# Two transformer blocks on one core: another order of the weight ring, and products placed ahead of two barriers

## The reference

```
first block:
  ada = silu(c) @ w_ada + b_ada -> shift, scale, gate     (three times 1024)
  p = (rms(x) * (1 + scale) + shift) @ w_in               (1024 x 3600)
  o_a = rms(gated_linear_attention(...)) * gla_norm_w * silu(a_gate)      4 heads
  o_b = rms(gated_linear_attention(...)) * hgrn_norm_w * silu(b_gate)     4 heads
  o_c = stick_breaking_attention(q, k, v) * silu(c_gate)                  4 heads
  x = rms(x + gate * (concat(o_a, o_b, o_c) @ w_out)) * final_norm_w
second block:
  h = rms(x) * norm_mix; projections by w_in_2 (1024 x 2824)
  att = rms(sliding_window_attention(att_q, att_k, att_v)) * norm_att_out
  hm  = rms(sigmoid(ml_gate) * mlstm(ml_q, ml_k, ml_v, ml_if)) * norm_ml_out
  x += concat(att, hm) @ w_out_2
  x += cross_attention(rms(x) * norm_cross, rms(mem) * norm_mem)
  x += mixture_of_experts(rms(x) * norm_ffn)              32 experts, top 2
  out = rms(x) * norm_final
```

## Time and profile before

| what | us |
|---|---|
| median of 3 runs (2258.09 to 2258.85) | 2258.72 |
| the profiled execution | 2257.62 |
| its span on the core | 2255.8 |
| PE busy, share of the span | 2114.3, 94% |
| DVE busy | 864.4 |
| ACT busy | 557.1 |
| POOL busy | 250.0 |
| mean granted TensorE clock, share of full | 0.975 |

### The profile page before, as it was taken

One profiled execution on the slowest core, in us unless ns is written; L12 is line 12 of the kernel. 1 busy time (PEld: TensorE's weight loads), 2 busy tenths in 40 slices (PEclk: granted clock), 3 DMA queues, 4 the chain that ended last, 5 costly groups with the idle time before them and its releaser, 6 DMA issues.

```text
span 2255.8 us, 38154 instructions
## 1 busy us (share of the span) xinstructions
PE 2114.3 (94%) x15824; PEld 1179.1 (52%) x15824; DVE 864.4 (38%) x1492; ACT 557.1 (25%) x1009; POOL 250.0 (11%) x252
## 2 busy tenths in 40 slices
PE   6999999999899989999989999999899999999996
PEld 4445555655334434654446454566566666665553
DVE  2225540545565730685446562134511111111115
ACT  3022322323563210342123211043011111111112
POOL 0013420433330000000000000000000000000002
PEclk9999999999899989999999999999799999999998
DMA  8212111101404042101110302100499999999996
GB/s 302 100 47 70 61 47 37 52 29 64 128 1 149 28 162 70 38 5 70 38 38 1 140 1 75 40 19 38 168 380 410 408 407 408 410 410 410 407 361 231
DMA packets 110277, 353.08 MB, mean 157 GB/s; under 512 B 18904, under 2 KB 59504, under 8 KB 97264
## 3 DMA queue, kind: packets, MB, share of 16 engines
q1 hardware_dynamic: 65168, 274.98, 31.6%
q0 software_dynamic: 14688, 54.53, 6.5%
q10 hardware_dynamic: 30336, 22.42, 3.1%
HBM read 310.75 MB, written 41.16 MB: 156 GB/s over the span
## 4 chain that ended last, share of the span: by engine, by line
PE 38%; DMA 11%; DVE 4%; issue 1%; ACT 1%; ACTq 0%; DVEq 0%; PEldq 0%
PE bank L598 17%; DMA y_of_slot<-HT 10%; PE bank L1173 8%; PE bank L1189 4%; PE bank L1007 2%; PE bank L654 1%; DVE work L1754 1%; DVE O L1760 1%; PE bank L1179 1%; PE bank L1164 1%; PE bank L1101 0%; PE bank L594 0%; ACTq L1682 0%; PE bank L981 0%; DVE work L1757 0%
## 5 line engine op out<-in xcount | busy, mean ns | idle before, releaser
L598 PE MATMUL bank<-slots,HT 128*128 128x512 f32 (+3 forms) x1088 | 372.0, 500 | 0.1
L598 PE MATMUL bank<-HT,slots 128*128 128x512 f32 x736 | 321.6, 599 | 3.8 <-PEq L588 1.3
L598 PEld LDWEIGHTS bank<-slots,HT 128*128 128x128 f32 x1088 | 190.1, 196 | 164.2 <-issue 160.8
L598 PEld LDWEIGHTS bank<-HT,slots 128*128 128x128 f32 x736 | 141.2, 192 | 181.9 <-issue 177.2
L1283 ACT ACTIVATE work<-bank 128x512 f32<-128x512 f32 (+5 forms) x205 | 108.6, 535 | 450.2 <-PE bank L598 271.9
L1283 ACT ACTIVATE work<-work 128x1024 f32<-128x1024 f32 (+7 forms) x199 | 158.6, 808 | 218.3 <-DVEq L143 158.2
L1283 ACT ACTIVATE HT<-bank 64x256 f32<-64x256 f32 (+2 forms) x218 | 92.8, 432 | 461.1 <-PE bank L1173 208.4
L1173 PE MATMUL bank<-slots,HT 128*32 128x256 f32 x3264 | 179.5, 379 | 2.8 <-DVE HT L2404 1.2
L2484 POOL TENSOR_TENSOR work<-work 128x1024 f32<-128x1024 f32 (+4 forms) x84 | 137.0, 1632 | 381.8 <-DVEq L143 322.0
L1173 PE MATMUL bank<-work,HT 128*32 128x256 f32 x3072 | 168.9, 379 | 0.6 <-DMA work<-in_w_e_up_dram 0.4
L1173 PEld LDWEIGHTS bank<-slots,HT 128*32 128x32 f32 x3264 | 107.6, 110 | 73.2 <-issue 6.8
(11 more groups left out here) (263 smaller groups left out, 2352.6 us busy)
## 6 DMA issues: line engine op xcount, KB each, us to landing
slots<-in_w_e_gate_dram SPq DMA_DIRECT2D x17, 2048.0 KB, 18.1
slots<-in_w_e_up_dram SPq DMA_DIRECT2D x17, 2048.0 KB, 22.8
slots<-in_w_e_down_dram SPq DMA_DIRECT2D x17, 2048.0 KB, 23.7
work<-in_w_e_gate_dram SPq DMA_DIRECT2D x16, 2048.0 KB, 18.2
work<-in_w_e_up_dram SPq DMA_DIRECT2D x16, 2048.0 KB, 22.9
work<-in_w_e_down_dram SPq DMA_DIRECT2D x16, 2048.0 KB, 23.8
slots<-in_w_in_dram SPq DMA_DIRECT2D x9, 2048.0 KB, 8.5
y_of_slot<-HT ACTq DMA_DIRECT2D x132, 96.0 KB, 24.5
```

The costliest lines, as they stand in the source:

```text
L598: ins = pe.matmul(bank, lhsT, rhs, start=(n == 0), stop=(n == len(pairs) - 1))
```

## The change

1. **Order of the weight ring.** c_qk goes ahead of ada4, ada5 goes behind a_gate, a_gate keeps its slot by two empty names (`a_gate_still`, `a_gate_last`), and all later chunks move on by one slot. PE makes the row product of ada5 after the barrier that follows linear attention a; ACT's copy of it, and the load of the gate row, move too.
2. **Values early.** V of the stick attention lies in the work area instead of HT and is loaded in one DMA right after the chunk stick_qk, ahead of out0.
3. **First mix.** ACT's Ln and Exp for the first two tiles' norms move ahead of the barrier. PE makes tile 0's out products before it turns tile 1, and hears from DVE that the stick gates are in.
4. **Queries ahead of two barriers.** The ringA fills (half 0) of att_q and of cross_q stand ahead of the last turned tile; the barrier is passed with these four banks full (`held=4`), and the ringV fills follow behind it.
5. **mLSTM.** Five of the eight first ml_gate products stand ahead of `emptied()`.
6. **Norm rows.** POOL issues both rows and the loads of x1 behind each other and waits afterwards.

```diff
@@ -293,16 +293,17 @@
         add_chunk("a_v", (w_in, 512, 1024))
-        for n in range(4, 6):
-            add_chunk(f"ada{n}", (w_ada, 512 * n, 512 * n + 512))
         add_chunk("c_qk", (w_in, 2576, 3088))
+        add_chunk("ada4", (w_ada, 512 * 4, 512 * 5))
         add_chunk("c_gate", (w_in, 3344, 3600))
         add_chunk("a_gate", (w_in, 1040, 1552))
+        add_chunk("ada5", (w_ada, 512 * 5, 512 * 6))
         add_chunk("b_qf", (w_in, 1552, 2064))
+
+        add_chunk("a_gate_still")
         add_chunk("b_v", (w_in, 2064, 2320))
-
-        add_chunk("a_gate_still")
         add_chunk("cv_bgate", (w_in, 3088, 3344), (w_in, 2320, 2576))
+        add_chunk("a_gate_last")
         ahead_dram = scratch("products_ahead", [P, 28 * HALF])
@@ -389,11 +390,13 @@
             qk = slots[:, n * NK * HALF:(n + 1) * NK * HALF]
-            Q, K, V = cut(qk[:, 0:2 * T], 2), cut(qk[:, 2 * T:4 * T], 2), HT[:, 4:6, :]
+            Q, K = cut(qk[:, 0:2 * T], 2), cut(qk[:, 2 * T:4 * T], 2)
...
             W = [[ar(HALF) for _ in range(2)] for _ in range(2)]
-            R = [[ar(HALF) for _ in range(2)] for _ in range(2)]
+            R = [[ar(HALF) for _ in range(2)]]
+            V = cut(ar(NT * 512), NT)[:, :, 256:512]
+            R.append([ar(HALF) for _ in range(2)])
             return Q, K, V, L, W, R
@@ -457,7 +460,7 @@
                   for n in range(2)]
-        GATE_CALLS = ((8, 12), (2, 4, 4), (2, 3, 3), (2, 3, 3), (0, 2, 0))
+        GATE_CALLS = ((3, 12), (2, 4, 4), (2, 3, 3), (2, 3, 3), (0, 2, 0))
         GATES_LATE = 6
@@ -582,8 +585,10 @@
-            def next_phase():
-                emptied()
+            def next_phase(held=0):
+
+                pe.wait_ge(ringA.free, ringA.filled - held)
+                pe.wait_ge(ringV.free, ringV.filled)
                 phases[0] += 1
@@ -736,7 +741,7 @@
                             if chunk == "a_gate":
-                                used("a_gate_still")
+                                used("a_gate_last")
                             ahead_over[name].append((pair, place))
@@ -820,12 +825,12 @@
-            for n in range(2):
-                row_product(f"ada{4 + n}", ringA)
+            row_product("ada4", ringA)
             emptied()
...
             next_phase()
+            row_product("ada5", ringA)
             product_fm("b_qf", 512, fm_fills(4))
@@ -851,13 +856,13 @@
                     if b == 2:
-                        pe.wait_ge(values_in, 32)
+                        pe.wait_ge(values_in, 16)
                     if at == 0 and x >= 2:
...
                     for hh in range(2):
-                        ins = pe.matmul(STICK_OUT[x % 2][64 * hh:64 * hh + 64, t0:HALF],
-                                        V[:, pair, j * P + 64 * hh:j * P + 64 * hh + 64],
+                        h = 2 * pair + hh
+                        ins = pe.matmul(STICK_OUT[x % 2][64 * hh:64 * hh + 64, t0:HALF], V[:, j, h * 64:h * 64 + 64],
                                         W[b % 2][hh][:, t0:HALF], start=(at == 0), stop=True, skip_group_check=True)
@@ -882,8 +887,9 @@
             turned = [ringA.filled]
+            hear("dve")
             for i in range(NT + 1):
-                if i + 1 < NT:
+                if 1 <= i and i + 1 < NT:
                     hear("dve")
@@ -893,13 +899,19 @@
                         used(name)
+                if i == 0:
+                    hear("dve")
+                    turn_tile(1, O[:, 1, :], ringA, SB0 // P)
+                    turned.append(ringA.filled)
+                if i == NT:
+                    product_fm("att_q", 512, [fill for fill in fm_fills(4) if fill[2] is ringA])
                 if i:
...
                     turn_tile(i - 1, NORMED[(i - 1) % 2], ringV)
-            next_phase()
-
-
-            product_fm("att_q", 512, fm_fills(4))
+            next_phase(held=4)
+
+
+            product_fm("att_q", 512, [fill for fill in fm_fills(4) if fill[2] is ringV])
             product_fm("att_kv", P, fm_fills(1))
@@ -973,7 +985,7 @@
             ringV.close(ins)
-            emptied()
+            pe.wait_ge(ringA.free, ringA.filled)
@@ -1010,6 +1022,8 @@
             ringA.use(banks[0:2])
+            gates_ahead(5)
+            emptied()
             maxima_of(0)
@@ -1062,24 +1076,26 @@
                         product_tm(name, 512, [(i, ringV)])
+                if i == NT:
+                    pe.wait_ge(ringA.free, ringA.filled)
+                    pe.wait_ge(ringD.free, ringD.filled)
+                    ringA.use(banks[0:4])
+                    product_fm("cross_q", 512, [fill for fill in fm_fills(4) if fill[2] is ringA])
                 if i:
...
                     turn_tile(i - 1, NORMED2[(i - 1) % 2], ringV)
-            emptied()
-            pe.wait_ge(ringD.free, ringD.filled)
-            ringA.use(banks[0:4])
-            next_phase()
+            next_phase(held=4)
...
             CQ, M2, MT, CK, CV, S, PT, OT = cross_area()
-            product_fm("cross_q", 512, [fill for fill in fm_fills(4) if fill[0] < 3])
+            product_fm("cross_q", 512, [fill for fill in fm_fills(4) if fill[2] is ringV and fill[0] < 3])
             hear("dve")
...
                 ringV.close(ins)
-            product_fm("cross_q", 512, [fill for fill in fm_fills(4) if fill[0] == 3])
+            product_fm("cross_q", 512, [fill for fill in fm_fills(4) if fill[2] is ringV and fill[0] == 3])
             emptied()
@@ -1427,14 +1443,15 @@
                     empty(lambda b: func(V[:, i, :], b, ACT.Copy))
-            for n in range(2):
+            def gate_of_block(n):
+
                 empty(lambda b: func(gate_row[:, n * P:(n + 1) * P], b[:, 0:P], ACT.Copy))
                 act.dma_start(gate_dram[n], gate_row[0:P:32, n * P:(n + 1) * P]).then_inc(gate_stored, 16)
+
+            gate_of_block(0)
             linear("a")
-            act.wait_ge(gate_stored, 32)
-            act.dma_start(gate_row, gate_dram.rearrange("a q n -> (a q n)").rearrange("(b n) -> b n", b=1)
-                          .partition_broadcast(P)).then_inc(gate_in, 16)
             next_phase()
+            gate_of_block(1)
@@ -1455,6 +1472,9 @@
                     empty(lambda b: func(V[:, i, 0:256], b[:, 0:256], ACT.Copy))
+            act.wait_ge(gate_stored, 32)
+            act.dma_start(gate_row, gate_dram.rearrange("a q n -> (a q n)").rearrange("(b n) -> b n", b=1)
+                          .partition_broadcast(P)).then_inc(gate_in, 16)
             linear("b")
@@ -1479,16 +1499,16 @@
                                 act.wait_ge(stored, 16 * 14)
+                        if x == len(SB_CHUNKS) - 1:
+                            hear("dve")
+                            do(rstd[:, 0:16], rstd[:, 0:16], ACT.Ln)
+                            do(rstd[:, 0:16], rstd[:, 0:16], ACT.Exp, scale=-0.5)
+                            tell("dve")
                         act.wait_ge(stick_out, x + 1)
...
-
-            hear("dve")
-            do(rstd[:, 0:16], rstd[:, 0:16], ACT.Ln)
-            do(rstd[:, 0:16], rstd[:, 0:16], ACT.Exp, scale=-0.5)
-            tell("dve")
@@ -2026,6 +2046,7 @@
             stick_gated(0)
+            tell("pe")
             mix_normed(1)
@@ -2586,9 +2607,9 @@
                 pool.dma_start(ROW2[:, at:at + 512], A[name].partition_broadcast(P)).then_inc(row_in, 16)
-                pool.wait_ge(row_in, 16 * (n + 3))
             for n in range(4):
                 pool.dma_start(X2[n], x1[2 * n:2 * n + 2].rearrange("i p d -> p i d")).then_inc(dma_in[n], 16)
+            pool.wait_ge(row_in, 64)
             CQ, M2, MT, CK, CV, S, PT, OT = cross_area()
@@ -2669,11 +2690,11 @@
                     at += hi - lo
-                if n == chunk_of["out1"]:
+                if n == chunk_of["stick_qk"]:
                     for x in range(2):
                         sp.wait_ge(stage_stored[x], 16 * 11)
-                    for k in range(2):
-                        sp.dma_start(cut(V[:, k, :], NT), B_AHEAD[:, :, k * P:(k + 1) * P]).then_inc(values_in, 16)
+                    sp.dma_start(V, B_AHEAD[:, :, 0:256]).then_inc(values_in, 16)
+                if n == chunk_of["out1"]:
                     for k in range(2):
...
                             .then_inc(b_gates_in, 16)
```

## The result

The changed kernel takes 2222.98 us in the median of 4 runs (2217.96 to 2227.62), the kernel before 2258.40 beside it: a ratio of 0.9852, 95% interval 0.9833 to 0.9872, about 35 us less. Run again later (the first experiment), 2224.94 and 0.985 (0.9833 to 0.9866). The forecast was 2217 with a range of 2210 to 2231: the time lies in the range, 6 us above the forecast.

What follows compares the result with a forecast made beforehand. PE was taken as the bound, busy 2114.3 of 2255.8 us. Terms summed to 41.8 us (27.9 waits, 13.9 clock): 2257.6 - 41.8 = 2215.8, with 1.1 for the median 2217; range 2210 to 2231 including rival 1.

Steps and rivals of the forecast that it cites:

- A: Linear attention a: c_qk ahead of ada4 removes PE's wait and slow records; 7.9 us, bounds 5.0 and 7.9.
- B: Barrier behind linear attention a: ACT no longer issues the gate row's load ahead of it; 0.3 us, bounds 0 and 0.4.
- rival 2: New ring: a_gate or b_qf lands late and PE waits, 9 us a piece; 2226 or 2235, chance 0.06.
- C: Stick stage: V loaded early removes 6.3 of PE's wait, plus 0.7 of clock; 7.0 us, bounds 5.3 and 9.1.
- D: Start of first mix: PE's wait moves to tile 2; 0 us, can cost 1.8 or gain 0.7.
- E: End of first mix: att_q fills ahead of the last turn remove wait and slow records; 11.2 us, bounds 7.5 and 11.2.
- F: Start of the mLSTM: five gate products fill PE's wait for DVE's copy, clock included; 8.5 us, bounds 4.3 and 9.0.
- G: Second mix: norm rows issued together shorten DVE's wait for the second row; 1.7 us, bounds 0 and 1.7.
- H: End of second mix: cross_q fills ahead of the last turn remove wait and slow records; 5.2 us, bounds 2.8 and 5.2.
- rival 1: Clock does not come back, new short waits may drop it elsewhere; only 27.9 us of waits gained, 2231; chance 0.14.
- Rivals 3 and 4: 3: fills held across both barriers delay other engines, 2272, chance 0.04; 4: edits fail to work, likely 2223, chance 0.08.

Runs made afterwards that it cites:

- the first experiment: The changed kernel run once more with nothing edited, as a control: 2224.94 us (2220.44 to 2229.65), ratio 0.985 to the kernel before.

## Why the prediction was right, and where it was off

The mechanism was right: PE is the bound, and filling its waits shortens the kernel by the wait and by the slow records behind it. The sum said 41.8; 35.8 came in the span and 33.8 up to the memory's keys, of which 0.8 is a start that was luckier. By its steps:

*A and B, the ring.* Said 8.2, came 9.8 - 1.65 = 8.15 in the pair of traces, and 6.4 to 6.9 against most others of the new ring. B gave 0.1 of its 0.3: without ACT's issue the barrier still took 1.20, so the 0.34 had not stood on top of it. The undone ring confirms the place and the slow records as priced, and no load came late (rival 2 is out: no DMA ends a wait between 163 and the stick stage).

*C, the values.* Said 7.0, came 5.96, and within its bounds. The clock term was right (0.7); the wait gave 5.3 instead of 6.3, since ACT takes up to 1.4 now, the come-back that the text named and then left out of the value taken. That wait was 1.33 to 1.40 in some traces and 0.36 in others; with 0.36, in the repeated run, the stage took 112.23 and the gain was 6.7. The step that was missing is that A alone also brings this gain.

*D, the start of the first mix.* Said 0, bounds -1.8 and +0.7; came -2.8, below the lower bound. The place was named rightly (the row of `b_ada`, tile 2, a new wait), and so was the danger: "it can cost 1.8 if the new wait of 3 to 4 us drops the clock". It did: 1.54 and 6.79 us in the fence above instead of 0.87 and 5.3, with 1.4 of it still there at the turn of tile 6. The value taken put this at nothing; undoing the order shows a cost of 1.9 to 2.4 us. The other 1.4 come from the row, which took 16.3 us to DVE instead of 14.8. In twelve traces with the old order of issues it took 14.4 to 14.9 us in seven and 15.7 to 16.5 in five: I took the duration of one execution for a constant. Where it took 14.4 to 14.5, with the new order, the wait was 3.8 to 3.9 us, as forecast.

*E, `att_q`.* Said 11.2, came 8.6 + 2.8 = 11.4, with the experiment 10.5. Right.

*F, the gate products.* Said 8.5, came 8.5, and the experiment gives 8.5. DVE kept up, as worked out.

*G, the norm rows.* Said 1.7, bounds 0 and 1.7; came 0.7, which is in the bounds, but the reason for the value taken failed: the text saw that the loads of x1 stand behind the rows in the same queue and priced that at nothing. With those loads behind it the second row needs 6.3 us, without them 4.6, and then DVE indeed goes on at ACT's root and PE gains 1.3 to 1.5 more.

*H, `cross_q`.* Said 5.2, came 4.8 in the pair of traces and 6.0 in the experiment, 0.8 above the bound. Right.

*The clock, rival 1.* I counted 13.9 us of clock, and PE's busy time fell by 14.2. That agreement is partly luck. The edits' own stretches gave it back (4.6 - 1.8 for the ring, then 0.7, 4.6, 4.0 and 2.1: 14.2), but in the changed kernel two stages without an edit lost 1.7 each, and the start, the routing and the experts gained 3.5, which no edit explains. So rival 1 was true in a small part, most of it in places that I had not named (D's is the one that I had): what looks like a stage of fixed length comes in two lengths. The window attention took 242.27 in one trace and 240.57 in another with the same count of instructions. The first fence is the changed kernel, the second the one with `cross_q` undone (us, busy PE, PEld, DVE, ACT, POOL, clock, DMA share, GB/s):

```profile
876.73:1119.00 242.27, 235.50 (x917) 119.52 (x916) 145.43 (x194) 63.36 (x83) 0.00 (x0) 0.99 0.10 35
...
1150.16:1223.56 73.40, 69.03 (x326) 44.72 (x327) 46.49 (x85) 22.75 (x43) 4.72 (x7) 0.98 0.13 44
```

```profile
877.16:1117.73 240.57, 233.81 (x917) 119.25 (x915) 145.43 (x194) 63.35 (x83) 0.00 (x0) 1.00 0.10 36
...
1148.90:1220.65 71.75, 67.39 (x327) 43.07 (x327) 46.57 (x86) 22.73 (x43) 4.72 (x7) 1.00 0.14 45
```

*Rivals 3 and 4.* Behind both barriers PE waits 1.35 us, not for 27: the held banks delay nobody that matters. No edit failed to do its work.

What the forecast lacks to the median, 6 us, as the traces share it out: D 2.8, the two slow steps 3.3, C 1.0, G 1.0, H 0.4, less the 0.8 of the start and some 2 of the last stages that nobody planned.

## What to carry to other kernels

Where one engine is full, fill its waits with products that are ready, across a barrier too if the banks can be held: the halves of part 4 and part 5 gave back waits of 7.5, 2.8 and 4.5 us and 3 to 4 us more each, nearly all of it clock. Ask too where the waiting goes that no product can fill: part 3 moved products ahead of a wait that a load sets, made one long wait of two short ones, and lost 1.9 to 2.4 us by it. Behind a filled wait ask which row or load is next, and read the order of DMA issues in its queue: what stands ahead of a small load or right behind it sets when it lands, and moving the row of `b_ada` ahead of 4 MB made that stage 6.6 us shorter, where PE's new order had made it longer. Two edits that both bring a load earlier may remove the same wait: undo them singly and together before giving each its price.
